# Silu on ScalarE in place of Tanh and a VectorE product for the short convolutions of a two-layer recurrent mixer

## What is computed

```python
def gdn_branch(q, k, v, b_logit, a_logit, z, conv_w, a_log, dt_bias, out_norm):
    qkv = jax.nn.silu(causal_dwconv(jnp.concatenate([q, k, v], axis=-1), conv_w)).astype(f32)
    q, k, v = jnp.split(qkv, [GDN_HEADS * GDN_DK, 2 * GDN_HEADS * GDN_DK], axis=-1)
    q = l2norm(q.reshape(b, s, GDN_HEADS, GDN_DK)) * (GDN_DK ** -0.5)
    k = l2norm(k.reshape(b, s, GDN_HEADS, GDN_DK))
```

## Time and profile before

| | us |
|---|---|
| median of 3 runs | 1980.58 |
| lowest to highest | 1978.45 to 1983.54 |
| the profiled execution | 1982.95 |
| its span, first to last instruction | 1981.1 |
| TensorE busy | 1940.0 (98%) |
| VectorE busy | 1470.9 (74%) |
| ScalarE busy | 1087.1 (55%) |
| mean granted TensorE clock | 0.996 of 2.4 GHz |

### The profile page before, as it was taken

The page is one execution under the profiler, slowest core; times in us unless marked ns, Lnnn a source line. Parts: engine busy times, 40 slices in busy tenths (PEclk is TensorE's granted clock), DMA queues, the critical chain, the costliest instruction groups (busy, mean ns, idle before and its releaser), DMA issues.

```text
span 1981.1 us, 35197 instructions
## 1 busy us (share of the span) xinstructions
PE 1940.0 (98%) x13137; PEld 1738.5 (88%) x13137; DVE 1470.9 (74%) x2252; ACT 1087.1 (55%) x1702; POOL 92.2 (5%) x61
## 2 busy tenths in 40 slices
PE   8999999999999999999999999999999999999999
PEld 7888889999888888889899988888888888888998
DVE  6777788677677777778677777777577888877887
ACT  5555664564555455556446644555345655765554
POOL 0000002010000000000120102000000000100000
PEclk9999999999999999999999999999999999999999
DMA  6556453344555655555424454565755665534654
GB/s 217 191 191 191 150 159 109 117 149 139 167 189 189 197 163 190 190 175 175 138 87 132 146 170 152 193 191 182 207 169 172 191 191 165 166 127 138 191 189 140
DMA packets 95793, 330.95 MB, mean 167 GB/s; under 512 B 10960, under 2 KB 16720, under 8 KB 95568
## 3 DMA queue, kind: packets, MB, share of 16 engines
q1 hardware_dynamic: 93712, 325.91, 51.7%
q10 hardware_dynamic: 1984, 3.68, 0.5%
HBM read 327.91 MB, written 1.64 MB: 166 GB/s over the span
## 4 chain that ended last, share of the span: by engine, by line
PE 83%; DVE 9%; DMA 3%; ACT 3%; issue 1%; POOL 1%; SPq 0%; ACTq 0%; DVEq 0%
PE ps L2145 81%; DVE w_lo L1210 3%; DMA raw<-stream 3%; ACT w_hi L556 1%; DVE arena L1569 1%; DVE x L1221 1%; POOL sc L1125 1%; PE ps L2376 1%; PE ps L2173 0%; PE ps L2590 0%; POOL tmp L1140 0%; DMA x<-x_in 0%; DVE tmp L1300 0%; DVE sc L1679 0%; DVE arena L1580 0%
## 5 line engine op out<-in xcount | busy, mean ns | idle before, releaser
L2145 PE MATMUL ps<-a_both,w_hi 128*128 128x256 f32 (+1 forms) x4864 | 993.3, 325 | 3.7 <-DVE w_lo L1210 1.7
L1210 DVE TENSOR_TENSOR w_lo<-raw,w_hi 128x1024 fp32r<-128x1024 f32 x614 | 749.0, 1225 | 265.4 <-ACT w_hi L556 264.9
L2145 PEld LDWEIGHTS ps<-a_both,w_hi 128*128 128x128 f32 x4864 | 814.3, 190 | 81.7 <-DVE w_lo L1210 4.1
L556 ACT ACTIVATE w_hi<-raw 128x1024 fp32r<-128x1024 f32 x614 | 637.0, 1052 | 162.5 <-DMA raw<-stream 100.5
L2145 PE MATMUL ps<-a_both,w_lo 128*128 128x256 f32 x3344 | 661.6, 283 | 0.0
L2145 PEld LDWEIGHTS ps<-a_both,w_lo 128*128 128x128 f32 x3344 | 524.8, 191 | 8.9
L2145 PE MATMUL ps<-w_hi,a_both 128*128 128x512 f32 (+2 forms) x1616 | 508.9, 385 | 11.8 <-DVE a_both L1325 6.5
L2145 PEld LDWEIGHTS ps<-w_hi,a_both 128*128 128x128 f32 x1616 | 302.3, 189 | 71.6 <-DVE a_both L1325 8.9
L2145 PE MATMUL ps<-w_lo,a_both 128*128 128x512 f32 (+2 forms) x808 | 309.7, 383 | 0.0
L2145 PEld LDWEIGHTS ps<-w_lo,a_both 128*128 128x128 f32 x808 | 153.4, 190 | 24.1
L1125 POOL TENSOR_TENSOR sc<-sc,nhalf 128x2 f32<-128x2 f32 (+5 forms) x25 | 63.2, 2529 | 1660.0 <-DVE sc L1249 1217.6
(11 more groups left out here) (333 smaller groups left out, 1237.1 us busy)
## 6 DMA issues: line engine op xcount, KB each, us to landing
raw<-stream SPq DMA_DIRECT2D x613, 512.0 KB, 3.5
arena<-upad SPq DMA_DIRECT2D x8, 284.0 KB, 5.9
gates<-late ACTq DMA_DIRECT2D x1, 1088.0 KB, 8.7
out<-tmp SPq DMA_DIRECT2D x8, 128.0 KB, 2.0
upad<-arena ACTq DMA_DIRECT2D x2, 288.0 KB, 8.1
con<-consts SPq DMA_DIRECT2D x1, 560.0 KB, 5.2
raw<-stream ACTq DMA_DIRECT2D x1, 512.0 KB, 3.9
x<-x_in SPq DMA_DIRECT2D x2, 256.0 KB, 5.0
```

The costliest lines, as they stand in the source:

```text
L556: nc.scalar.activation(w_hi[:, u % SLOTS, :], raw[:, u % RAW, :], ACT.Copy).then_inc(hi_ready, 1)
L1210: V.tensor_tensor(w_lo[:, u % SLOTS, :], raw[:, u % RAW, :], w_hi[:, u % SLOTS, :], ALU.subtract).then_inc(split_ready, 1)
L2145: return nc.tensor.matmul(o, a, b, start=start, stop=stop, **k)
```

## The change

ScalarE computes Silu itself, in place in `y`: Silu(2y) with y = c/2 is Silu(c). The buffer `yth` and VectorE's `silu(p)` go, with the step `silu` of VectorE; the semaphore `silu_th` is renamed `silu_ready` and counts ScalarE's own instructions, on which the Square waits. The places in ScalarE's program stay.

```diff
-DVE_STEPS = (["z0", "cvar", "g", "cumcp", "gld", "silu", "c_lo", "gvar", ...
+DVE_STEPS = (["z0", "cvar", "g", "cumcp", "gld", "c_lo", "gvar", ...
...
-        yth = reg(7168, 12, TOK)
...
                 def th(p):
                     act.wait_ge(conv_ready, 6 * l + p + 1)
-                    nc.scalar.activation(yth[:, 2 * p:2 * p + 2, :], y[:, 2 * p:2 * p + 2, :], ACT.Tanh).then_inc(silu_th, 1)
+                    v = y[:, 2 * p:2 * p + 2, :]
+                    nc.scalar.activation(v, v, ACT.Silu, scale=2.0).then_inc(silu_ready, 1)
...
                 moba_split(1, 2)
-                act.wait_ge(*DV.at(l, "silu"))
+                act.wait_ge(silu_ready, 6 * l + 6)
                 nc.scalar.activation(flat(tmp[:, :, :]), flat(y[:, 0:8, :]), ACT.Square).then_inc(*AC.sig(l, "gsq"))
...
-                def silu(p):
-                    dve.wait_ge(silu_th, 6 * l + p + 1)
-                    v = y[:, 2 * p:2 * p + 2, :]
-                    i = V.scalar_tensor_tensor(v, yth[:, 2 * p:2 * p + 2, :], 1.0, v, ALU.add, ALU.mult)
-                    if p == 5:
-                        i.then_inc(*DV.sig(l, "silu"))
-                    else:
-                        tick(i)
                 latents(-1)
                 for p in range(6):
                     u = POS["gdn", l] + 2 * p
                     split(u + AHEAD); split(u + 1 + AHEAD)
                     conv(p)
-                    if p:
-                        silu(p - 1)
                     latents(p)
...
                 moba_split(0)
-                silu(5)
                 dve.wait_ge(*AC.at(l, "c_hi"))
```

More of the change, by code:

```diff
@@ L235 @@
             + ["u", "wT", "S1", "ob0", "wS", "oa", "mobakT", "ob1", "mobaT", "oT", "qT0", "qT1", "kT0", "kT1"])
-DVE_STEPS = (["z0", "cvar", "g", "cumcp", "gld", "silu", "c_lo", "gvar", "Et", "A", "X0", "kgd", "vb", "XT0", "QK", ("X", 1), ("T", 1), "mobavar"]
+DVE_STEPS = (["z0", "cvar", "g", "cumcp", "gld", "c_lo", "gvar", "Et", "A", "X0", "kgd", "vb", "XT0", "QK", ("X", 1), ("T", 1), "mobavar"]
              + [s for s in LV_STEPS if s[0] != "U" and 1 < s[1] < LEVELS - 1] + ["mobaqk", ("T", LEVELS - 1)]
@@ L297, in build @@
         loop_chain = sem("loop_chain")
-        cb_ready, conv_ready, silu_th = sem("cb_ready"), sem("conv_ready"), sem("silu_th")
+        cb_ready, conv_ready, silu_ready = sem("cb_ready"), sem("conv_ready"), sem("silu_ready")
         z_th, zs_ready, m_ready, gate_evac = sem("z_th"), sem("zs_ready"), sem("m_ready"), sem("gate_evac")
```

## The result

The changed kernel took 1991.35 us (median of 6, 1989.62 to 1994.91), the kernel before, beside it on the same chip, 1982.99 us (median of 6, 1978.45 to 1983.97): a ratio of 1.0047, 95% interval 1.0034 to 1.0059. It is 8.4 us slower, above the 5.9 us that can be told from no change, and above the range. The profiled execution of after took 1991.2 us with a span of 1989.4 us, so it stands for the median.

A forecast was written before the change was run, and what follows sets the result against it. TensorE, busy 98% of the span, was taken to bound the kernel. Plus 1.3 us of longer waiting and 0.8 of clock, +2.1 on the median 1980.58, gave 1982.7 us; range 1975.5 to 1988.0.

The forecast's parts named there:

- Loads: ScalarE: four table loads a layer, eight in all, ahead of Silu p0, line 769, Silu p4 and line 796; 1.35 us each.
- The rival in which a switch costs twice its row: ScalarE empties before each load, so a switch costs 2.7 us: about 1988 us; chance 0.04.
- the one without a switch: Silu shares the set of Exp and Tanh, so VectorE's relief counts: 1975 to 1978.5 us; chance 0.18.
- loads two and three: Ahead of line 769 and Silu p4: 2.7 us less 1.78 idle, 0.9 us later in the first layer, nothing in the second.
- The rival in which the waits cannot be filled: ScalarE's idle times move along, three loads a layer reach the Square in full: 1990.3 us; chance 0.08, 1985.5 to 1991.
- VectorE's relief: Twelve products of line 1580 go, 8.2 us of VectorE; worth 0 to minus 3.2 us on the end.
- Load one: Ahead of Silu p0: delays p2's copies and the taps by 1.35 us, mostly absorbed; 0.4 us carried through.
- Load four: Ahead of the Exp of line 796: 2.3 us of cover before TensorE turns `A`, 1.35 used; costs nothing.
- The clock: TensorE's clock after the first layer's longer wait: between 0 and 1.6 us, half taken, 0.8 us.
- The sentence under what would prove it wrong: Prediction wrong if ScalarE's named idle times keep their size or any TensorE wait outside these stages moves over 1 us.

The follow-up runs named there:

- the alike kernels: Profiled kernels alike for TensorE up to the turn of `A`: three like the kernel before, four like the changed kernel; Square waits 0.27 to 2.06 us.
- both kernels with the later GpSimd: GpSimd's first two products wait until `kgd` is written: in the changed kernel, 1987.02 us; in the kernel before with only Load four added, 1983.85 us.
- the filled wait: Changed kernel with eight unused 128x512 matmuls put into TensorE's wait for the Square: 1988.48 us, ratio 1.0028 against the kernel before.

## Why the prediction was right and wrong

**Loads: right.** Eight, at the four lines, 1283 ns each. ScalarE of after in order of time, first layer; compare:

```profile
264.58 1.28 ACT L769 ACT_TABLE_LOAD   x1
265.88 0.21 ACT L769 ACTIVATE sc<-sc 128x8 f32<-128x8 f32 x1
266.00 0.19 ACT L771 ACTIVATE sc<-sc 128x4 f32<-128x4 f32 x1
266.09 2.01 ACT L555 ACTIVATE w_hi<-raw 128x1024 fp32r<-128x1024 f32 x2
...
269.33 1.28 ACT L748 ACT_TABLE_LOAD   x1
270.63 0.63 ACT L748 ACTIVATE arena<-arena 128x512 f32<-128x512 f32 x1
...
273.70 2.01 ACT L555 ACTIVATE w_hi<-raw 128x1024 fp32r<-128x1024 f32 x2
275.60 1.91 ACT L790 ACTIVATE tmp<-arena 128x2048 f32<-128x2048 f32 x1
```

From the load's start to the Exp or Silu are 1.30 us. Two neighbours without a load between overlap by some 0.1 us, so a load puts its follower off by a little more: the Exp of line 796 starts 6.93 us ahead of the turn of `A` before and 5.53 after, 1.40 us later where the sum had 1.35. The rival in which a switch costs twice its row is out; so is the one without a switch. The three idle times that were to take loads two and three (before 266.99, 272.62 and 274.69) are gone, and with only these two loads on the path the wait before the statistics is 0.6 us and none, against none in either layer with all hidden: 0.6, where the sum had 0.9. The rival in which the waits cannot be filled is out too: of three loads a layer, 3.9 us, the Square's wait shows +0.65 and -0.51. That its time, 1990.3 us, lies near the measured 1991.35 is chance.

**VectorE's relief: right in kind.** Line 1580 is gone. In the stretch 240.4 to 275.6, the same place in after, VectorE is busy 31.7 of 35.2 us, where "below 31" was foretold: one split and three small products more than in the earlier trace rows fell into it.

**Load one: mis-sized.** The sum carried 0.4 us. VectorE of after, first layer:

```profile
252.15 2.36 DVE L1210 TENSOR_TENSOR w_lo<-raw,w_hi 128x1024 fp32r<-128x1024 f32 x2 [1.81 <-ACT w_hi L555]
```

VectorE, full in this stage before, stands still 1.81 us for a ScalarE that is a load late, right after it has won its first products back. By then one product is saved, 0.69 us, against a load of 1.28. Counted from the start of the stage, this split begins 11.57 us in, where before it began 10.36 us in (251.64 less 241.28): nearly all of the load comes through. The stages behind it take back a part (the statistics start 0.65 later), but with no other load on the path it still costs 0.26% (0.9996 against 0.9970). For the wait that the prediction summed, one pair of profiles is thin: by the means of the alike kernels it grew by 1.2 us in the first layer (0.70 to 1.88) and fell by 0.2 in the second (1.40 to 1.17), close to the 1.3 and 0 that the prediction had.

**Load four: the step that failed.** The prediction said "Nothing", by 2.3 us of cover between `A` and its turn. That cover was read correctly; the load uses it, and TensorE turns `A` without waiting. But `A` is only the first thing that the late VectorE makes, and the step looked at what is queued behind the load on ScalarE, not at what is queued behind `A` on VectorE: the mask products, three weight splits, then `kgd`. These are VectorE's rows of before, first layer:

```profile
295.02 1.22 DVE L1210 TENSOR_TENSOR w_lo<-raw,w_hi 128x1024 fp32r<-128x1024 f32 x1
...
298.19 2.35 DVE L1210 TENSOR_TENSOR w_lo<-raw,w_hi 128x1024 fp32r<-128x1024 f32 x2
300.46 0.69 DVE L1648 TENSOR_TENSOR arena<-ps,sc 128x512 f32<-128x512 f32 x1
301.07 0.68 DVE L1649 TENSOR_TENSOR arena<-ps,sc 128x512 f32<-128x512 f32 x1
```

`kgd` is written at 301.75, and TensorE starts on what follows it at 302.18 while its previous product still drains to 302.43:

```profile
300.38 2.05 PE L2145 MATMUL ps<-arena 128*128 128x128 f32 x16 [0.18 <-ACT gates L804]
302.18 0.48 PE L2145 MATMUL ps<-a_both,w_hi 128*128 128x256 f32 x2
```

That is 0.4 to 0.7 us of cover, not 2.3. These rows were in the trace of before. Of after:

```profile
291.07 1.06 ACT L555 ACTIVATE w_hi<-raw 128x1024 fp32r<-128x1024 f32 x1 [9.72 <-PE ps L2134]
292.15 1.28 ACT L796 ACT_TABLE_LOAD   x1
293.44 2.45 ACT L796 ACTIVATE gates<-gates,sc 128x128 f32<-128x128 f32 x8
```

```profile
295.93 2.16 DVE L1627 SCALAR_TENSOR_TENSOR gates<-ps,sc,gates 128x128 f32<-128x128 f32 x8 [6.41 <-ACT gates L796]
...
302.31 2.32 DVE L1210 TENSOR_TENSOR w_lo<-raw,w_hi 128x1024 fp32r<-128x1024 f32 x1
...
304.55 0.68 DVE L1637 TENSOR_TENSOR arena<-ps,sc 128x512 f32<-128x512 f32 x1
```

Counted from the turn of `A`, the end of `A` is 1.42 us later than before (0.88 instead of 2.30 us ahead of it) and the end of `kgd` (line 1638, at 305.83) 2.52 us later (6.86 instead of 4.34 behind it). The 1.10 between these is one row: the second split takes 2.32 us instead of 1.22. GpSimd of before, then of after:

```profile
300.40 2.59 POOL L1140 TENSOR_TENSOR tmp<-gates,con 128x512 f32<-128x512 f32 x2 [15.87 <-ACT gates L804]
```

```profile
301.95 3.81 POOL L1140 TENSOR_TENSOR tmp<-gates,con 128x512 f32<-128x512 f32 x2 [16.54 <-ACT gates L804]
```

GpSimd waits for ScalarE's copy of the turned `A`, which follows TensorE, and TensorE did not get later. VectorE did. From the turn of `A` to GpSimd's start are 2.99 and 2.98 us. Before, the last split ended (300.54) just as GpSimd began (300.40); now the second lies inside GpSimd's two products. Both pay: VectorE 1.10, GpSimd 1.22. The cover is the 0.68 us from 301.75 to 302.43, less some 0.05 from the end of `kgd` (305.83) to TensorE's start (305.88), and with the rounding of the rows 0.62. TensorE waits 2.52 less 0.62 of cover, 1.90:

```profile
305.88 0.51 PE L2134 MATMUL ps<-a_both,w_hi 128*128 128x256 f32 x2 [1.90 <-DVE arena L1638]
```

and without the collision 1.42 less 0.62, 0.80, which is what both kernels with the later GpSimd show. The Trainium skill ("SBUF — State Buffer", "Who interferes with whom") has a rule for this: a VectorE instruction with two SBUF inputs contends with a GpSimd instruction that reads SBUF, one with a single SBUF input does not (outside VectorE's 2-port modes), and whoever comes second blocks until the other is done. The rows agree: the split (two inputs in SBUF) and line 1650 (likewise) grow, by 1.10 and 0.99; the `kgd` and `vb` products, which read PSUM, keep 0.68 and 0.69 us beside GpSimd. Line 1649, also with two inputs in SBUF, keeps its 0.69 us too; it starts at 306.39, where GpSimd's first product (305.22 and 1.31 us long alone) is about to end. As an estimate, a split that begins at 302.31, blocked until GpSimd's first product (301.95, 1.31 us alone) is done, would end 1.22 later, at 304.5; if the first split, which runs to 302.39, held GpSimd's product back before, at 304.9. It ended at 304.63. That blocking is the form of the collision is not shown beyond this; that the two collide is.

**The clock: right in sign, mis-sized, and in one place of three.** The sum took 0.8 us, within the 1.6 that the two layers' statistics differ, and in the first layer alone. Measured are 3.25 us in the middle stretches, 1.61 of them in the first layer, and 1.49 in the third. In the middle stretch the loss lies in the statistics and the 32 matmuls behind them; the four `moba` units at its end, before and after, take the same:

```profile
286.40:297.41 11.01, 11.01 (x51) 9.05 (x50) 6.51 (x13) 5.42 (x11) 0.00 (x0) 1.00 0.31 98
287.98:298.97 10.99, 10.99 (x51) 9.05 (x50) 4.58 (x11) 6.69 (x12) 0.00 (x0) 1.00 0.29 95
```

The middle part is borne out by the filled wait and by the table beside it (+2.4 and +1.2 us by the means). The third stretch fell below the full clock only behind a wait for `kgd` of 1.9 us, and then in four of eight cases (14.25 us; 12.76 in the others, at 1.00); behind 0.8 us (11.66) it kept 1.00 in all four. Filling that wait was not tried. What stays open is which idle time costs which step: 21.43 and 23.03 us both followed a wait of 1.93 us in the same layer of the same instructions. The length of the wait alone does not say.

**The sum, with the measured terms.** Predicted: +1.3 waiting for the Square, 0 for load four, +0.8 clock, +2.1. Measured in the profiled pair: +0.14, +3.80, +4.74, and 0.52 beyond the wait for `kgd` at the full clock, less 0.90 elsewhere, +8.30. The prediction added its sum to 1980.58; the kernel before, beside after, took 1982.99, so 2.4 us of the distance to the forecast of 1982.7 are the base, and 1991.35 would lie outside the range with that base too. The sentence under what would prove it wrong, a wait outside the named stages that moves by over 1 us, is the one that came true, by `kgd`. (Three more waits for VectorE moved so in this pair: line 1325 from 6.5 to 3.8 us, line 1221 from 5.9 to 7.0 and line 2010, 2021 of before, from 0.2 to 1.4. They are scatter: over the other twelve kernels the first two spread from 3.9 to 6.2 and from 5.4 to 8.2, and the third is at most 0.6.) In the medians load four alone costs 6.1 us, and the changed kernel takes 0.77%, some 15 us, more than its form with the loads hidden: the clock makes such terms larger than the waits behind them.

## What to carry to other kernels

List the table loads that a new function brings, and put each into an idle stretch of ScalarE by a one-column activation, or move the small activations of the other set there: the same change went from 0.47% slower to 0.30% faster. When a step is delayed, cover is not read at its first reader but at every later product of each engine that reads it, down that engine's queue to the point at which someone waits; and a shifted engine has to be laid over its neighbours again, as its work may now meet theirs. And a wait of 1 to 2 us of TensorE is to be priced with the clock of the stretch behind it, in the profiled pair 4.74 us beside 3.94 us of waits; as it changes from execution to execution, one profile does not give that price.

## What the runs showed of the hardware

- A split on VectorE (two fp32 sources in SBUF, 128x1024) took 2.32 us instead of 1.22 beside two GpSimd products of 128x512, and these 3.81 instead of 2.59 us; products with a source in PSUM were not slowed.
- The granted clock of the middle stretch, in which TensorE never stood still, was .91 to .78 behind waits of 0.3 to 2.2 us, .91 or 1.00 without a wait, and .91 and .84 behind a filled one: 18.0 to 23.1 us for the same matmuls, and up to one step of 1.6 us apart in executions of the same instructions.
- Silu shares no table set with Exp here: four switches a layer in program order, two where the calls were grouped. Each load took 1283 ns, and its activation followed 1.30 us after its start; an Exp behind one came 1.40 us later than without it.
